# Sums of squares of the state-space tiles: six adds move from GpSimd to VectorE, to the head of the next tile's output step

## The reference, cut to what matters

```
y = y + d_skip * x_in
y = y.reshape(bsz, length, M2_WIDTH) * silu(z)
yg = y.reshape(bsz, length, M2_GROUPS, M2_WIDTH // M2_GROUPS)
yg = yg * lax.rsqrt(mean(yg * yg, axis=-1) + EPS)
y = yg.reshape(bsz, length, M2_WIDTH) * norm_w
h = h + concatenate([out_a, y]) @ w_out
```

## Time and profile before

| what | us |
|---|---|
| median of 3 runs (1767.07 to 1770.04) | 1768.79 |
| the profiled execution | 1769.76 |
| its span, first to last instruction | 1767.9 |
| PE busy | 1739.9 (98%) |
| DVE busy | 1172.4 (66%) |
| ACT busy | 717.3 (41%) |
| POOL busy | 11.8 (1%) |

### The profile page before, as it was taken

How to read it: one execution, slowest core, us unless ns; L and a number is a source line. 1 busy time by engine, 2 the same in 40 slices (tenths; PEclk the granted TensorE clock), 3 DMA queues, 4 the chain that set the end, 5 groups by cost and what they waited for, 6 DMA issues and landing times.

```text
span 1767.9 us, 27352 instructions
## 1 busy us (share of the span) xinstructions
PE 1739.9 (98%) x11022; PEld 1530.2 (87%) x11022; DVE 1172.4 (66%) x1809; ACT 717.3 (41%) x1101; POOL 11.8 (1%) x12
## 2 busy tenths in 40 slices
PE   9999999999999999999999999999998999999997
PEld 7877887788888888888899999999998999999885
DVE  6666656566568777734577767788797877777332
ACT  6433433332353333333545454544454433333221
POOL 0000000000000000000000000000000000000000
PEclk9999999999999999999999999999999999999999
DMA  6222232223333333333222222222122233333331
GB/s 203 82 73 78 77 88 91 84 73 97 95 96 96 98 100 99 97 96 99 78 74 73 69 73 63 62 75 80 60 73 68 76 96 96 96 92 89 108 95 60
DMA packets 44716, 153.81 MB, mean 87 GB/s; under 512 B 6032, under 2 KB 6416, under 8 KB 44592
## 3 DMA queue, kind: packets, MB, share of 16 engines
q1 hardware_dynamic: 44592, 152.08, 28.4%
HBM read 149.96 MB, written 2.10 MB: 86 GB/s over the span
## 4 chain that ended last, share of the span: by engine, by line
PE 80%; DVE 11%; ACT 4%; DVEq 2%; issue 1%; ACTq 1%; DMA 0%; SPq 0%; POOL 0%
PE ps L678 79%; DVE arena L1421 3%; ACT arena L1031 2%; DVE w_lo L1418 2%; DVEq L1970 1%; DVE arena L1428 1%; PE ps L682 1%; ACTq L1401 1%; ACT w_hi L1031 1%; DVE arena L1418 1%; DVE h_res L1418 1%; DVE u_lo L1638 0%; ACT L1036 0%; DVE arena L1435 0%; DVE r_bc L1418 0%
## 5 line engine op out<-in xcount | busy, mean ns | idle before, releaser
L678 PE MATMUL ps<-u_hi,w_hi 128*128 128x258 f32 (+3 forms) x2376 | 639.7, 323 | 1.4 <-DVE arena L1421 1.2
L678 PE MATMUL ps<-u_lo,w_hi 128*128 128x258 f32 (+3 forms) x2376 | 631.0, 319 | 0.4 <-DVE u_lo L1638 0.3
L678 PE MATMUL ps<-u_hi,w_lo 128*128 128x258 f32 (+3 forms) x2368 | 631.3, 320 | 0.0
L1418 DVE TENSOR_TENSOR w_lo<-w_raw,w_hi 128x1024 fp32r<-128x1024 f32 (+1 forms) x280 | 341.4, 1219 | 150.4 <-ACT w_hi L1031 139.0
L678 PEld LDWEIGHTS ps<-u_hi,w_hi 128*128 128x128 f32 (+1 forms) x2376 | 392.2, 188 | 41.2 <-issue 5.1
L678 PEld LDWEIGHTS ps<-u_lo,w_hi 128*128 128x128 f32 (+1 forms) x2376 | 393.9, 188 | 33.9 <-DVE u_lo L1638 1.3
L678 PEld LDWEIGHTS ps<-u_hi,w_lo 128*128 128x128 f32 (+1 forms) x2368 | 391.2, 188 | 31.2 <-issue 0.2
L1031 ACT ACTIVATE w_hi<-w_raw 128x1024 fp32r<-128x1024 f32 (+1 forms) x281 | 294.1, 1047 | 297.5 <-PE ps L678 290.3
L1428 DVE SCALAR_TENSOR_TENSOR ffn<-full,par,ffn 128x512 f32<-128x512 f32 (+2 forms) x176 | 132.2, 751 | 80.9 <-ACT ffn L1031 77.7
L1031 ACT ACTIVATE arena<-arena 128x528 f32<-128x528 f32 (+11 forms) x189 | 96.2, 531 | 217.3 <-DVE arena L1421 86.4
L1031 ACT ACTIVATE ffn<-full,par 128x512 f32<-128x512 f32 x88 | 67.7, 769 | 268.7 <-DVE full L1421 268.7
(11 more groups left out here) (160 smaller groups left out, 1509.4 us busy)
## 6 DMA issues: line engine op xcount, KB each, us to landing
w_raw<-weights SPq DMA_DIRECT2D x278, 512.0 KB, 3.5
h_res<-xT SPq DMA_DIRECT2D x8, 256.0 KB, 5.4
outT<-h_res SPq DMA_DIRECT2D x6, 256.0 KB, 2.4
cst<-consts SPq DMA_DIRECT2D x1, 730.0 KB, 8.8
w_raw<-weights SPq DMA_DIRECT2D x2, 256.0 KB, 4.1
outT<-ffn SPq DMA_DIRECT2D x2, 256.0 KB, 2.6
seg<-consts SPq DMA_DIRECT2D x1, 256.0 KB, 8.6
par<-params SPq DMA_DIRECT2D x1, 240.0 KB, 6.9
```

What stands on the lines that cost most here:

```text
L678: return nc.tensor.matmul(out, lhsT, rhs, start=start, stop=stop)
L1418: return V.tensor_tensor(out, a, b, op)
```

## The change

The six adds leave GpSimd's program. VectorE gets a function `add_square(t)` of the same add, with a wait for `sq`. It is called at the head of `ssm_c(t + 1)`, ahead of that function's wait for `C`, and for the last tile at the end of `ssm_gate(7)`. The semaphore `added`, its count and its waiters are as before. The waits of the adds for each other fall away, as VectorE issues them all.

```diff
         @block.gpsimd
-            def ssm_sq(t):
-                if t % 4 == 0:
-                    return
-                pool.wait_ge(ssm_sem["sq"], t + 1)
-                if t % 4 > 1:
-                    pool.wait_ge(ssm_sem["added"], 3 * (t // 4) + t % 4 - 1)
-                total = m_sq[:, t // 4, USED:]
-                nc.gpsimd.tensor_tensor(total, total, m_z[t % 2][:, USED:], ALU.add).then_inc(ssm_sem["added"], 1)
...
-            for kind, i in STEPS:
-                if kind == "ssm_sq":
-                    ssm_sq(i)
             last_tiles()
...
+            def add_square(t):
+
+                if t % 4 == 0:
+                    return
+                dve.wait_ge(S["sq"], t + 1)
+                total = m_sq[:, t // 4, USED:]
+                tt(total, total, m_z[t % 2][:, USED:], ALU.add).then_inc(S["added"], 1)
+
             def ssm_c(t):
+                if t:
+                    add_square(t - 1)
                 dve.wait_ge(S["C"], t + 1)
...
                 half_mul(m_y[:, t, USED:], m_y[:, t, USED:], gate).then_inc(S["gated"], 1)
+                if t == M2_T - 1:
+                    add_square(t)
```

## The result

The changed kernel took 1774.90 us in the median of six runs (1772.62 to 1775.52), the kernel before 1767.93 beside it (1766.96 to 1770.04): a ratio of 1.0036, 95% interval 1.0024 to 1.0049. That is 6.4 us by the ratio and 7.0 between the medians. The profiled execution took 1775.02 us with a span of 1773.2, that of before 1769.76 and 1767.9. Of the 5.3 us, 0.37 was there before any of the six adds had an effect (TensorE's first `ac_st` row of the stage starts at 1203.61 in place of 1203.24), and 0.8 arises behind the last VectorE instructions, which start 4.48 later than before.

The account below looks back on a forecast made before the run. TensorE's waits, work or clock were taken to set the time, with VectorE nearly full and leading from `a 5`. Terms 6.6 + 2.8 - 1.4 - 0.3 - 2.0 + 1.4 - 0.6 = +6.5 us gave 1775.3 us, range 1771.8 to 1778.2.

Parts of the forecast that it names:

- Sum 0 waits for the third add, +6.6: TensorE at sum 0: starts at 1282.9 in place of 1276.30, waiting for VectorE's add ahead of `c 4`, +6.6 us.
- The clock behind it, +2.8: TensorE behind sum 0: low clock after the wait loses +2.8 us, bounded by nothing and 5.0.
- The old wait at `a 5` goes, -1.4: TensorE at `a 5`: the wait for ScalarE's root of group 0 disappears, -1.4 us.
- ScalarE's lag, -0.3: ScalarE at `a 5`: it no longer starts 0.40 us behind TensorE because of older work, -0.3 us.
- Two collisions, -1.0 and -1.0: VectorE at 1307.94 and 1337.02: two stalls beside GpSimd adds go, -1.0 us each.
- Adds 5 and 6, +0.7 each: VectorE ahead of `c 6` and `c 7`: the adds of tiles 5 and 6 now run there, +0.7 us each.
- The last add, -0.6: At sum 1: square of tile 7 to start of sum takes 0.8 us on VectorE in place of 1.39, -0.6 us.
- Adds 1 and 2, nothing: VectorE ahead of the third add: these adds, about 0.73 us each, disappear in its later waits, costed at nothing.
- signs named to look for: Trace after: among others, granted clock 0.50 for some 6 us behind sum 0; wait at sum 1 still 3 to 4 us.
- slower still: Rival: clock stays low longer or drops again at `a 7`; +9 to +11 us, 1778 to 1780; chance 0.09.
- the same: Rival: TensorE's waits of 1.1 and 3.4 us after `a 5` swallow the delay; 1769.2 to 1771.8 us; chance 0.12.
- faster: Rival: sum 0 does not wait, only the part behind counts; -1.2 us, 1767.6 us; chance 0.05.

Follow-up runs that it names:

- experiment 1: Kernel before with only the add of tile 3 moved to VectorE, at the head of `c 4`: 1774.55 us, ratio 1.0038 to the kernel before.
- experiment 2: Changed kernel with only the add of tile 3 given back to GpSimd, the five others on VectorE: 1765.92 us, ratio 0.9987 to the kernel before.
- experiment 3: Changed kernel with VectorE's add of tile 3 earlier, ahead of the v2 parts behind `b 4`: 1768.76 us, ratio 1.0003 to the kernel before.
- experiment 6: Changed kernel with TensorE's sum 0 moved behind the groups om (0,0) and om (0,1): 1768.10 us, ratio 1.0002 to the kernel before.
- Experiment 5: Changed kernel with six more TensorE matmuls, results overwritten, ahead of the wait at sum 0: 1772.32 us, ratio 1.0023 to the kernel before.
- experiment 8: Kernel before with only add 7 moved to VectorE, the five others on GpSimd: 1767.62 us, ratio 0.9995 to the kernel before.
- experiment 7: Changed kernel with adds 1, 2 and 3 back on GpSimd, 5, 6 and 7 on VectorE: 1768.49 us, ratio 1.0001 to the kernel before.
- experiment 4: Changed kernel with VectorE's add of tile 3 moved to the head of its `a 4`: 1767.27 us, ratio 0.9996 to the kernel before.
- experiment 9: As experiment 4, but without add 7; TensorE sums tile 7's square itself: 1765.73 us, ratio 0.9989 to the kernel before.
- experiment 10: Changed kernel with add 3 on GpSimd, 1, 2, 5, 6 on VectorE, tile 7's square summed by TensorE: 1766.77 us, ratio 0.9988 to the kernel before.

## Why the prediction was right, step by step

- **Sum 0 waits for the third add, +6.6.** It came as +6.63, with the add at 1282.19 where the prediction had 1282.16. To the hundredth that is luck: this execution came 0.37 late to the stage, and VectorE made up 0.35 at mz 4. The prediction said that nothing ahead of the add waits for something that has moved; the evacuation of mz 4 does (its row has `ssm_added`), and its gap fell from 0.51 to 0.16. Counted from the first `ac_st` row of the stage, sum 0 is 6.26 late, and 6.69 in experiment 1, where adds 1 and 2 are on GpSimd. Experiments 1, 2 and 3 show by three edits that the place of this add is the whole of the loss, and experiment 6 that the price is paid by what stands behind TensorE's wait.
- **The clock behind it, +2.8.** Too high by a little in this execution. Before, at full clock, TensorE had ended om (0,1) 7.09 after the start of sum 0; now it took 9.42, so 2.33 was lost. The trace had no wait of 6 us, and the value taken was that of the 3.43 us one. Experiment 5 gives 2.3 to 2.6 in the whole times. In experiment 1 the same way of counting gives 9.94 - 7.09 = 2.85, behind a wait of 6.62. The other way to put it, that the loss grows with the wait (up to 5.0; its own 0.6 per us gives 4.7), is not borne out: waits of 6.20 and 6.62 cost 2.33 and 2.85, and the one of 3.43 cost 2.8.
- **The old wait at `a 5` goes, -1.4.** It did. 6.63 + 2.33 - 1.43 is the 7.53 that TensorE was late there, where the prediction had 8.0.
- **ScalarE's lag, -0.3.** ScalarE came to `a 5` 7.20 late (1293.61 against 1286.41), a lag of 0.33 gone, and VectorE 6.89 late, another 0.31 gone that the prediction had not seen.
- **Two collisions, -1.0 and -1.0.** -1.01 and -1.02, and experiment 8 puts them back. The Trainium skill's rule on them ("SBUF — State Buffer", section "Who interferes with whom") agrees with these rows. It agrees too where VectorE was first: the slab's low part on VectorE began at 1202.33 and lasted 1.23, and GpSimd's add at 1202.99 took 1.72. The other page of the Trainium skill that was weighed ("Perfetto Trace Analysis", section "Optimizing GPSIMD Operations") holds for five of the six adds taken together (experiment 2) and fails for the third: engine for engine VectorE is the faster one for it, 0.69 against the 1.72 at 1253.92, and the kernel lost 6 to 7 us by it. A third collision was not counted: beside GpSimd's add 2, at 1224.84, three rows of a convolution on VectorE took 3.26 us, and 2.37 without it (first before, then after). These 0.89 us disappear in a wait that VectorE has behind them.

```profile
1224.78 3.26 DVE L1428 SCALAR_TENSOR_TENSOR arena<-arena,par 128x527 f32<-128x527 f32 x3
```

```profile
1225.76 2.37 DVE L1416 SCALAR_TENSOR_TENSOR arena<-arena,par 128x527 f32<-128x527 f32 x3
```

- **Adds 5 and 6, +0.7 each.** VectorE goes on 0.61 after the start of an add, as behind the add at 1282.19, so +0.6 each.
- **The last add, -0.6.** From the start of the square to sum 1 it was 2.02 and is 1.41 (1356.52 to 1357.93): -0.61.
- **Adds 1 and 2, nothing.** Right for what they cost: sum 0 comes at the same time with them and without (experiment 7). TensorE is 0.37 late at 1203 and still 0.36 at 1260, so they cost it nothing up to there. That VectorE is 0.35 earlier at mz 4 without GpSimd's was missed. In experiment 2 this brings the root of sum 0 0.34 earlier; in the change, where nobody waits for that root, it brings the third add earlier by as much.

Taken from VectorE's 6.89 on: -1.01, +0.61, -1.02, +0.61, -0.61, and the 0.32 by which VectorE waited longer for ScalarE at `a 7` (0.51 in place of 0.19, with the clock low there), make 5.8, and sum 1 starts 5.79 late. The prediction had 7.7 at VectorE's `a 5` and 6.5 here: it was 0.8 too high at the start of the stretch, 1.2 with the 0.37 taken off, and right behind it to 0.1.

That its 6.5 lies so near the 6.4 to 7.0 of the runs is in part luck. The mechanism was right, but in the pair of profiles from which it was reckoned the sum would have been 1.1 too high at sum 1 (5.79 less 0.37 is 5.4). What stands behind sum 1, where it put no change, took off another 1.4: from sum 1 to the norm it was 37.26 us before, with the low clock, and 35.86 after, without. The medians bring that back, since the profiled execution of before lay 1.8 above its median and that of after 0.1.

Two of the signs named to look for were wrong. The wait at sum 1 did not stay at 3 to 4 us, it fell to 1.79: the clock dropped once more, at `a 7`, behind a wait of 1.72, and TensorE lost about (1 - 0.72) x 6.0 = 1.7 us there by the granted clock, and 1.5 by its rows (8.35 us from `a 7` to the small matmuls at 1343.90, in place of 6.81). That is the second drop of the rival "slower still", and the reason given against that rival held: TensorE had the wait at sum 1 to pay it from. The wait became 1.64 shorter (3.43 - 1.79); that this is nearly the same number is chance, since TensorE made up 0.6 on the way from there to sum 1, and sum 1 starts 0.7 less late than `a 7` (5.79 against 6.49). And the granted clock behind sum 0 was 0.61 over 6.4 us, not 0.50.

The rival "the same" failed as argued. TensorE's waits behind `a 5` could swallow none of it, since VectorE led there. The rival "faster" asked for a sum 0 that does not wait, and that is experiment 2: with the sum not waiting the kernel is faster, by 1.8 us in the profiles and 2.2 in the medians, where it said 1.2, which the interval holds too.

## What to carry to other kernels

Before work is moved to a faster engine, look where that engine is in its list at the moment when the result is wanted: the 0.69 us on VectorE ended at 1282.9, and the 1.72 us on an idle GpSimd at 1255.6, where TensorE wanted the result at 1276.3. What such a wait costs is what stands behind the waiting instruction: with 6 us of matmuls put ahead of the sum the same late add cost nothing that the times can tell. And of a bundle of like edits each wants its own sum, since here five brought about 2 us (experiment 2) and the sixth by itself cost 6.4 (experiment 1).

## What the runs showed of the hardware that was not expected

**Equal waits of TensorE are followed by the low clock in one execution and not in another.** At `a 5` the wait is 1.09 in experiments 2 and 4 (also 1.09 in 9 and 1.08 in 10). The stretch behind it, first of experiment 2, then of experiment 4:

```profile
1284.00:1292.00 8.00, 6.82 (x55) 6.40 (x56) 7.29 (x16) 7.56 (x25) 0.00 (x0) 1.00 0.23 78
```

```profile
1284.00:1292.00 8.00, 7.09 (x44) 6.67 (x45) 7.29 (x17) 7.59 (x24) 0.00 (x0) 0.79 0.21 71
```

The same 8 us, 55 matmuls against 44, and the clock at 1.00 against 0.79; experiments 9 and 10 had 0.79. A wait of 1.43 was followed by 0.79 before and in experiment 7, and by 1.00 in experiment 8. At `a 7` a wait of 1.74 was followed by a mean of 0.92 over 1328 to 1350 in experiment 2 and by 1.00 in experiments 3 and 6. At sum 1 a wait of 3.02 to 3.04 was followed by 1.00 in experiment 3 and by 0.72 over the next 6 us in experiments 4 and 6; behind the 3.47 of experiment 1 the low clock came 1.4 us later than behind the 3.43 of before. So the length of a wait alone does not set its price by the clock, which was here between nothing and 2.9 us, and it can move a whole time by about as much. What decides it was not tested.

**TensorE's pace differed by 1% at the same granted clock.** In a stage that no edit touches, 100 us of back-to-back matmuls, first experiment 2, then experiment 4 (columns: us, busy and matmuls of PE, PEclk, DMA share, GB/s):

```profile
1400.00:1500.00 100.00, 100.00 (x844) 1.00 0.32 96
```

```profile
1400.00:1500.00 100.00, 100.00 (x836) 1.00 0.32 96
```

Of the twelve profiled executions those of experiments 3, 4 and 10 ran at 836, the others at 843 or 844. It is not that records are missing: between 1410 and 1450 the rows of two matmuls start 0.24 us apart throughout in experiment 4, and 0.23 to 0.25 apart in experiment 2. In an earlier stage, 1000 to 1100, before and experiments 3 and 4 all have 870. From the norm behind sum 1 to the last weight matmul experiment 3 took 368.40 us and before 366.08, so 2.3 us more, and that is where experiment 3 lost its lead; between experiments 4 and 2 it is 2.2. Whether it belongs to the kernel or to the execution is open.
